# Second block's output projection: four of its second-pass units put before the last first-pass units

## What is computed

```python
        mix = jnp.concatenate([rmsnorm(oa, out_gain_a[l]),
                               rmsnorm(ob, out_gain_b[l]),
                               rmsnorm(oc, out_gain_c[l])], axis=-1)
        x = x + jnp.einsum('bse,ed->bsd', mix, w_o[l])
        h = rmsnorm(x, norm_mlp[l])
        u = jax.nn.relu(jnp.einsum('bsd,df->bsf', h, w_up[l]))
        x = x + jnp.einsum('bsf,fd->bsd', u * u, w_down[l])
```

## Time and profile before

| | |
|---|---|
| time, median of 3 runs | 3318.18 us (3317.75 to 3319.74) |
| span of the profiled execution | 3316.8 us |
| PE busy | 3277.0 us, 99% |
| DVE busy | 2170.4 us, 65% |
| ACT busy | 1629.2 us, 49% |
| POOL busy | 953.4 us, 29% |
| TensorE clock, mean share granted | 0.997 |

### The profile page before, as it was taken

How to read it: one execution, slowest core, us unless ns; L and a number is a source line. 1 busy time by engine, 2 the same in 40 slices (tenths; PEclk the granted TensorE clock), 3 DMA queues, 4 the chain that set the end, 5 groups by cost and what they waited for, 6 DMA issues and landing times.

```text
span 3316.8 us, 48563 instructions
## 1 busy us (share of the span) xinstructions
PE 3277.0 (99%) x19112; PEld 2845.6 (86%) x19112; DVE 2170.4 (65%) x3028; ACT 1629.2 (49%) x2740; POOL 953.4 (29%) x863
## 2 busy tenths in 40 slices
PE   8999999999999999999999999999999999999998
PEld 7888888888888888788888888888778888888887
DVE  5668577654676557778764467555778775457654
ACT  4457554443444445555444344444655544344443
POOL 2434233210132224256320023112327431013221
PEclk9999999999999999999999999999999999999999
DMA  7544546755555554555555555555355555555554
GB/s 250 193 155 151 177 146 204 235 188 193 186 190 189 194 172 139 163 167 172 190 195 183 194 185 190 191 194 174 123 173 174 183 189 190 195 184 191 191 193 144
DMA packets 188283, 604.60 MB, mean 182 GB/s; under 512 B 36597, under 2 KB 41573, under 8 KB 188054
## 3 DMA queue, kind: packets, MB, share of 16 engines
q1 hardware_dynamic: 188054, 601.47, 54.6%
HBM read 599.16 MB, written 8.00 MB: 183 GB/s over the span
## 4 chain that ended last, share of the span: by engine, by line
PE 83%; DVE 8%; ACT 4%; POOL 3%; issue 2%; DMA 0%; DVEq 0%; POOLq 0%; ACTq 0%; SPq 0%
PE ps L1717 82%; DVE wl L2321 4%; ACT wh L2059 1%; POOL xr L2667 1%; ACT sS L2155 1%; POOL tB L2667 1%; DVE sS L2325 1%; DVE x L2329 1%; ACT sS L2144 1%; PE ps L1720 1%; DVE sS L2332 0%; ACT tA L2059 0%; DVE den L2463 0%; DVE tB L2321 0%; DVE xr L2321 0%
## 5 line engine op out<-in xcount | busy, mean ns | idle before, releaser
L2321 DVE TENSOR_TENSOR wl<-wt,wh 128x1024 fp32r<-128x1024 f32 (+2 forms) x1104 | 1474.3, 1367 | 320.9 <-ACT wh L2059 305.2
L1717 PE MATMUL ps<-x,wh 128*128 128x512 f32 x4448 | 1572.9, 398 | 15.6 <-DVE x L2329 14.1
L1717 PE MATMUL ps<-x,wl 128*128 128x256 f32 x4448 | 1244.7, 280 | 0.0
L2059 ACT ACTIVATE wh<-wt 128x1024 fp32r<-128x1024 f32 (+2 forms) x1104 | 1111.8, 1047 | 249.5 <-PE ps L1717 210.6
L1717 PEld LDWEIGHTS ps<-x,wh 128*128 128x128 f32 x4448 | 836.5, 188 | 213.9 <-DVE wl L2321 10.0
L1717 PEld LDWEIGHTS ps<-x,wl 128*128 128x128 f32 x4448 | 841.7, 189 | 0.6
L1717 PE MATMUL ps<-ua,wh 128*128 128x512 f32 (+1 forms) x2432 | 836.6, 389 | 5.1 <-DVE xr L2321 5.1
L2321 DVE TENSOR_TENSOR tB<-ps,tA 128x256 f32<-128x256 f32 x470 | 195.1, 422 | 735.1 <-ACT tA L2059 734.7
L1717 PE MATMUL ps<-ua,wl 128*128 128x256 f32 x2368 | 662.9, 280 | 0.0
L2059 ACT ACTIVATE tA<-ps 128x256 f32<-128x256 f32 x470 | 176.5, 380 | 978.1 <-PE ps L1717 973.1
L1717 PEld LDWEIGHTS ps<-ua,wh 128*128 128x128 f32 x2432 | 452.1, 188 | 104.9 <-DVE xr L2321 5.0
(11 more groups left out here) (233 smaller groups left out, 1819.1 us busy)
## 6 DMA issues: line engine op xcount, KB each, us to landing
wt<-in_w_up SPq DMA_DIRECT2D x384, 512.0 KB, 4.3
wt<-in_w_down SPq DMA_DIRECT2D x384, 512.0 KB, 4.7
wt<-in_w_in SPq DMA_DIRECT2D x156, 512.0 KB, 4.6
wt<-in_w_o SPq DMA_DIRECT2D x64, 512.0 KB, 4.5
wt<-in_w_out SPq DMA_DIRECT2D x32, 512.0 KB, 4.3
wt<-in_w_vb SPq DMA_DIRECT2D x16, 512.0 KB, 4.3
wt<-in_w_va SPq DMA_DIRECT2D x16, 384.0 KB, 3.7
wt<-in_w_vsl SPq DMA_DIRECT2D x8, 512.0 KB, 6.1
```

The costliest lines, as they stand in the source:

```text
L1717: return eng.matmul(o, l, r, start=start, stop=stop, skip_group_check=True)
L2059: return eng.activation(o, i, ACT.Copy, **kw)
L2321: return eng.tensor_tensor(o, a, b, op)
```

## The change

The 16 units stand in another order. Before: 0 to 15. Now: 0, 1, 2, 3, 4, then 8, 9, 10, then 5, 11, 12, 6, 13, 14, 7, 15. The weights are loaded in the same new order. `finish(gens)` is called ahead of every second-pass unit. Only the first of these calls finds work left, and it stands behind unit 4 instead of behind unit 7. No instruction is added or taken away.

```diff
+O2_UNITS = [0, 1, 2, 3, 4, 8, 9, 10, 5, 11, 12, 6, 13, 14, 7, 15]
...
-        for u in range(16):
+        for u in O2_UNITS:
             add_feed("w_o2", l, u)
...
-        for u in range(8):
-            unit([(True, True, residual(st, 2 * u + g, False, scale=True)) for g in range(2)], 8, UA(0))
-        finish(gens)
-        for u in range(8):
-            last_w = unit([(True, True, residual(st, 2 * u + g, True, G_MLP2 + 16 * l, x2free=[last_in],
-                                                 last=(lambda: norm_T(st)) if 2 * u + g == 15 else None))
+        for u in O2_UNITS:
+            if u < 8:
+                unit([(True, True, residual(st, 2 * u + g, False, scale=True)) for g in range(2)], 8, UA(0))
+                continue
+            finish(gens)
+            o = 2 * u - 16
+            last_w = unit([(True, True, residual(st, o + g, True, G_MLP2 + 16 * l, x2free=[last_in],
+                                                 last=(lambda: norm_T(st)) if o + g == 15 else None))
                            for g in range(2)], 8, UA(8))
```

## The result

| | before | changed |
|---|---|---|
| time, median | 3320.03 us (15 runs, 3314.52 to 3325.87) | 3326.43 us (15 runs, 3322.13 to 3330.87) |
| ratio, 95% interval | | 1.0024 (1.0017 to 1.0031) |
| span of the profiled execution | 3316.8 us | 3326.7 us |

What follows compares the result with a forecast made beforehand. PE, busy 99% of the span, was taken to bound the kernel. Branch B's norm in one piece 10.2 us, minus 5.3 gained at the projection's end, plus 2.0 for clock drops: 6.9 on 3318.2, so 3325.1 us (range 3318.5 to 3330.5).

Steps and rivals of the forecast that it cites:

- The sums wait 1.85 us: Behind unit 4, PE waits 1.85 us for POOL's last squares before the sums of branch B's norm.
- The round trip, of which PE idles 1.04 us: Behind the sums, DVE, POOL, PE's spread and DVE's copy take 2.2 us uncovered; PE idles 1.04 us of it.
- Four tiles on DVE in 3.7 us: Behind the spread, DVE readies branch B's four tiles in 3.7 us, not 4.6, as POOL has nothing to do.
- Two or three waits for `ua` of 0.8 and 1.0 us: In the eight pairs behind the spread, PE waits for tile slots, mostly 0.8 us (first) and 1.0 us (third).
- Join 5.1 us a layer without the clock: Running branch B's norm in one piece behind unit 4 costs 5.1 us per layer, 6.0 with longer scalings.
- A drop in each layer, 1.0 us each: PE's idles behind unit 4 likely lower the clock to half in each layer, costing 1.0 us each, 2.0 us together.
- Tile 14 comes 1.5 us earlier (1.0 to 1.9) and 0.6 in layer 1: At the projection's end DVE catches up, shortening the MLP's wait by 1.5 us in layer 0, 0.6 in layer 1.
- The drop at the MLP of layer 0, 3.16 us, goes: With about 0.5 us of wait left at the MLP's start, layer 0's half clock disappears, winning 3.16 us.
- the join mostly hidden: Rival: branch B's norm behind unit 4 costs only 2.0 us per layer, no clock drop; 3316.9 us, chance 0.10.
- the end not helped: Rival: the wait at the MLP's start stays because POOL has unit 7's operations first; 3330.4 us, chance 0.07.
- The case without a drop: Rival: as forecast, but no clock drop behind unit 4, 2.0 us less; 3323.1 us, chance 0.22.
- the one with full drops: Rival: 6.8 us of half clock after PE resumes behind unit 4, 2 x 3.16 us; 3329.4 us, chance 0.16.

Runs made afterwards that it cites:

- join alone: Kernel before with its unit order kept, only the call emptying the background work moved from behind unit 7 to behind unit 4; 3330.11 us, ratio 1.0031.
- only unit 7 late: Kernel before with only unit 7 moved, between units 14 and 15, background work emptied behind unit 6; 3317.77 us, ratio 0.9994.
- one split less ahead: Kernel before, but each second-block MLP's first unit splits one half of the next unit's weights ahead, not two; 3317.21 us, ratio 0.9994.

## Why the prediction was right, step by step

- **The sums wait 1.85 us:** 1.76 to 1.78 in all six joins. **The round trip, of which PE idles 1.04 us:** 1.04 in all six.
- **Four tiles on DVE in 3.7 us** and not in 4.6, because POOL has nothing to do: from 1487.95 to 1490.62 + 0.82 = 1491.44 it is 3.5 us. Two scalings took 0.88 us where they took 1.39 beside a working POOL, and POOL stood idle for 5.68 us. The choice between the two ends was right.
- **Two or three waits for `ua` of 0.8 and 1.0 us:** the step was off. At full clock there are two, of 0.54 and 0.69 us; at half clock there are none or one, up to 0.30 us.
- **Join 5.1 us a layer without the clock:** the last step of unit 4 to the ninth pair is 1.93 us to the sums and 6.82 behind them, 8.75 less the 3.55 of before, so 5.2 us. It was the term that decided, and it held.
- **A drop in each layer, 1.0 us each:** the drops came in five joins out of six. They cost 0.94, 0 and 0.84 us in layer 0 and 0.21, 0.01 and 0.31 in layer 1, on average 0.8 us for both instead of 2.0. This term was too large, because in layer 1 the drop was half as long and in layer 0 it stayed away once. The argument that it passes beside waits anyway was right.
- **Tile 14 comes 1.5 us earlier (1.0 to 1.9) and 0.6 in layer 1:** this term was too small. The waits fell from 2.0 to 0 to 0.18 us and from 1.09 to 0 to 0.17 us. DVE began 1.46 us earlier, as forecast, and lost 0.27 of it on ACT; but the two splits took 2.52 us and not the 3.32 of the earlier trace rows that I had kept, another 0.8 us. `x` began 2.0 us earlier behind PE's end. The cause was only in part the one given: the prediction put all of this down to unit 7 having no `x` splits, and the join alone, without unit 7 moved, takes off about as much of the wait.
- **The drop at the MLP of layer 0, 3.16 us, goes:** it went, and its price was right (3.13 us between two traces of the kernel before). But it stood in only two of three traces of before, so it is worth 2.1 us in a mean over runs. That the idle of 1.1 us at the MLP of layer 1 does not lower the clock held in all three.
- **Sum:** 10.4 + 0.8 - (1.9 + 1.0 + 2.1) = 6.2 us, where I had 10.2 + 2.0 - 5.3 = 6.9. The corrected spans differ by 3306.2 - 3298.9 = 7.3 us, the medians by 6.4. The clock at the join was put 1.2 us too dear, the waits at the end 0.8 us too low and the drop there 1.1 us too high, so the errors partly cancel. The forecast is within 1.4 us of the median, and that owes something to this and to luck: it was added to 3318.2 us, the median of three runs, where fifteen gave 3320.03. As a difference, 6.9 us stand against 6.4 by the medians and 8.0 by the ratio.

Of the rivals, the join mostly hidden and the end not helped are refuted by the rows above (8.75 us against 3.55, and no wait at the MLP). Join alone and only unit 7 late show the two parts of the change each by itself: by their ratios 10 us lost (7 to 14) and 2 us won (5 won to 1 lost). They don't add up term by term, since each of them alone takes off half of the wait at the MLP or more, and in the trace of neither does a drop follow it; the 10 us of the join alone are net of that. The case without a drop and the one with full drops differ from the forecast by less than executions do, and each was seen at a single join or in none: 3.2 us behind a join never occurred.

Open: that in the corrected spans 1.1 us more is found than in the sum. The changed traces have short drops elsewhere (at 1225.9, 504.6 and 1228.3 us, 3.4 us each) which those of before lack; whether the change brings these about, a thousand instructions away, or chance does, three traces can't tell. For chance speaks that such a drop of 3.4 us stands at 505.9 us in the kernel with one split less ahead too, whose units stand in the old order.

## What to carry to other kernels

Work that is spread between matmuls is cheap because each step of its round trip between engines has cover; if it is run in one piece, each of its waits is paid, and what is queued behind it on the slowest of its engines can be paid as well (in the join alone, the additions that free a bank). Before reordering matmuls to let a lagging engine catch up, look at what stands in its queue ahead of the late operation: one weight split moved behind the `x` splits shortened the stretches as much as moving unit 7 did (4.6 and 0.9 us against 3.1 and 0.7), without touching the norm; in the whole time neither can be told from no change. Where a stage is judged from one trace, take the stretch between two instructions that all versions have, and two or three traces, since a clock drop of 3 us may belong to the execution and not to the kernel. And a stall can pay something back: while PE stood, the lagging DVE caught up, so the price of a stall and the wait that it spares further on have to be read together.

## What the runs showed of the hardware that was not expected

- PE has two paces at full granted clock for the same pairs, 0.347 and 0.353 us, 579 and 568 matmuls in 100 us. It keeps one for hundreds of us; 846 to 1078 us of the slower one were seen in three executions of the same kernel, which is a difference of 4.4 us. What switches it was not found. At the slower pace DVE keeps up better: the wait at the MLP of the kernel before is 1.98 to 2.04 us at the faster and 1.07 to 1.10 us at the slower one. In the kernel before the second projection runs at the slower pace up to the MLP (2597 us) in all three traces; in the changed kernel the pairs behind the join of that layer were at the faster one in two traces of three.
- Half-clock periods lasted 3.4 or 6.8 us, wherever they stood away from the program's end. An idle of 1.98 to 2.04 us was followed by one in two of three cases; idles of 1.77 and 1.04 us, 0.6 us of work apart, by 6.8 us, 3.4 us or none (3, 3 and 2 of the eight joins of the changed kernel and of join alone). The Trainium skill (TensorE: Matmul & The Clock Gate, What's actually happening) states that a block on the chip sets the granted share of the clock by how busy PE has been of late. The traces agree in that each drop at a join or at the MLP came with an idle of PE; they add that the same stall can end in different ways.
- DVE took longer where POOL was at work: two `qb` scalings 0.88 us beside an idle POOL and 1.39 beside a working one; two weight splits 2.52 us in the changed kernel, where POOL stood still when the second began, and 3.32 before, where it was at work beside both.
